# Rotary positions: swapping partitions by transfers from SBUF to SBUF in place of products with a permutation matrix

## What is computed

```python
def apply_rope(t, cos, sin):
    half = t.shape[-1] // 2                      # 32 of the head's 64 channels
    t1, t2 = t[..., :half], t[..., half:]
    return jnp.concatenate([t1 * c - t2 * s_, t2 * c + t1 * s_], axis=-1)

def layer(x, l):
    x = x + 0.5 * rms_norm(swiglu(rms_norm(x, pre1), w_in1, w_out1), post1)
    u = rms_norm(x, mix_pre)
    dq, dk, dv, dz, db, da, sq, sk, sv, gate_a, gate_b = split(u @ mix_w_in)
    y_a = deltanet_branch(dq, dk, dv, dz, db, da, ...)
    y_b = swa_sink_branch(sq, sk, sv, sinks, cos, sin)      # applies apply_rope to sq and sk
    merged = sigmoid(gate_a) * (y_a @ w_branch_a) + sigmoid(gate_b) * (y_b @ w_branch_b)
    x = x + rms_norm(merged @ mix_w_out, mix_post)
    return x + 0.5 * rms_norm(swiglu(rms_norm(x, pre2), w_in2, w_out2), post2)
```

## Time and profile before

| | |
|---|---|
| median of 3 runs | 2424.35 us (2422.82 to 2425.39) |
| the profiled execution | 2424.42 us |
| its span | 2422.6 us |
| granted clock of TensorE, mean | 0.972 |
| TensorE, VectorE, ScalarE, GpSimd busy | 95%, 51%, 32%, 5% |

### The profile page before, as it was taken

How to read it: one execution, slowest core, us unless ns; L and a number is a source line. 1 busy time by engine, 2 the same in 40 slices (tenths; PEclk the granted TensorE clock), 3 DMA queues, 4 the chain that set the end, 5 groups by cost and what they waited for, 6 DMA issues and landing times.

```text
span 2422.6 us, 31002 instructions
## 1 busy us (share of the span) xinstructions
PE 2306.3 (95%) x12232; PEld 1900.0 (78%) x12232; DVE 1225.3 (51%) x1641; ACT 781.7 (32%) x1272; POOL 113.8 (5%) x104
## 2 busy tenths in 40 slices
PE   8999997999899899999899999979998998999997
PEld 6888885788787788888788888857787877888885
DVE  5555325864446565552365553359534465554523
ACT  4333223522443333332243232234134333332321
POOL 0000000131000000000000000002300000000000
PEclk9999998999999999999999999989899999999998
DMA  4332332211122233333222333322111232323332
GB/s 163 97 97 98 99 104 96 66 41 55 51 70 87 105 104 96 96 99 103 84 87 92 99 103 97 104 87 62 45 54 44 79 101 85 117 89 104 104 96 87
DMA packets 58716, 214.79 MB, mean 89 GB/s; under 512 B 6512, under 2 KB 6512, under 8 KB 58096
## 3 DMA queue, kind: packets, MB, share of 16 engines
q1 hardware_dynamic: 57744, 203.82, 26.4%
q0 software_dynamic: 864, 9.44, 1.1%
HBM read 206.94 MB, written 6.29 MB: 88 GB/s over the span
## 4 chain that ended last, share of the span: by engine, by line
PE 73%; issue 15%; DVE 8%; ACT 2%; DMA 1%; POOL 0%; POOLq 0%; DVEq 0%; SPq 0%; ACTq 0%
PE ps L461 22%; PE ps L463 21%; PE ps L462 21%; PE ps L668 1%; DVE tmp L1189 1%; DVE x L1195 1%; DVE wlo L1145 1%; DMA raw<-in_wstream_dram 1%; PE ps L656 1%; PE ps L497 1%; DVE tmp L1343 1%; DVE tmp L1168 1%; ACT whi L850 0%; PE ps L764 0%; PE ps L729 0%
## 5 line engine op out<-in xcount | busy, mean ns | idle before, releaser
L461 PE MATMUL ps<-uhi,whi 128*128 128x512 f32 x2144 | 856.3, 399 | 38.9 <-DVE ulo L1150 18.9
L1145 DVE TENSOR_TENSOR wlo<-raw,whi 128x1024 fp32r<-128x1024 f32 (+1 forms) x384 | 465.9, 1217 | 806.2 <-ACT whi L850 799.1
L462 PE MATMUL ps<-ulo,whi 128*128 128x512 f32 x2144 | 844.7, 394 | 0.0
L463 PE MATMUL ps<-uhi,wlo 128*128 128x512 f32 x2144 | 844.4, 394 | 0.0
L850 ACT ACTIVATE whi<-raw 128x1024 fp32r<-128x1024 f32 (+1 forms) x384 | 397.7, 1040 | 843.6 <-PE ps L463 740.5
L461 PEld LDWEIGHTS ps<-uhi,whi 128*128 128x128 f32 x2144 | 409.0, 191 | 133.0 <-issue 27.2
L463 PEld LDWEIGHTS ps<-uhi,wlo 128*128 128x128 f32 x2144 | 408.6, 191 | 87.3
L462 PEld LDWEIGHTS ps<-ulo,whi 128*128 128x128 f32 x2144 | 409.5, 191 | 83.7 <-issue 0.5
L461 PE MATMUL ps<-hhi,whi 128*128 128x512 f32 x704 | 273.9, 389 | 0.0
L462 PE MATMUL ps<-hlo,whi 128*128 128x512 f32 x704 | 273.9, 389 | 0.0
L463 PE MATMUL ps<-hhi,wlo 128*128 128x512 f32 x704 | 273.9, 389 | 0.0
(11 more groups left out here) (215 smaller groups left out, 1602.0 us busy)
## 6 DMA issues: line engine op xcount, KB each, us to landing
raw<-in_wstream_dram SPq DMA_DIRECT2D x371, 512.0 KB, 3.5
raw<-in_wstream_dram SPq DMA_DIRECT2D x16, 256.0 KB, 2.6
x_home<-x POOLq DMA_DIRECT2D x2, 2048.0 KB, 8.0
x<-x_home POOLq DMA_DIRECT2D x2, 2048.0 KB, 8.7
x<-in_xT_dram SPq DMA_DIRECT2D x4, 512.0 KB, 6.7
out_dram<-x SPq DMA_DIRECT2D x8, 256.0 KB, 2.0
rcs<-in_rope_dram POOLq DMA_DIRECT2D x2, 512.0 KB, 9.9
con<-in_con_dram SPq DMA_DIRECT2D x1, 612.0 KB, 9.2
```

What stands on the lines that cost most here:

```text
L461: pe.matmul(o, lh, bhi, start=first, stop=False)
L462: pe.matmul(o, lh, blo, start=False, stop=False)
L463: return pe.matmul(o, ll, bhi, start=False, stop=last)
L1145: dve.tensor_tensor(wlo[:, s, 0:cols], raw[:, s % RAWS, 0:cols], whi[:, s, 0:cols].bitcast(f32), ALU.subtract) \
```

## The change

The step `rope` leaves TensorE and PSUM. In its place GpSimd issues four transfers per tile ahead of its multiplication by the cosines. Each takes 32 partitions of the tile to the 32 partitions that they change places with, in `tmp` 2 or 3, and counts up a new semaphore, `turned`. VectorE waits for all four and multiplies `tmp` by the sines in place. Since `tmp` 2 and 3 hold the squares of `lst` until then, GpSimd waits for the last of these sums (`l_stat`) ahead of tiles 0 and 1. The signs move into the table of sines. The table of constants loses 128 columns.

```diff
@@ banks_of
-    if k == "rope":
-        return (2 + x % 2,) if x < 4 else (5,)
@@ trunk
+        turned = [sem("turned0", 64 * 3), sem("turned1", 64 * 2)]
@@ TensorE
-                    elif k == "rope":
-                        i, b = step[1], banks_of(step)[0]
-                        use(L, step, b)
-                        pe.wait_ge(tile_read.h, tile_read.at(L, TILE_M + (16 if i < 4 else 17)))
-                        done(pe.matmul(bank(b), con[:, K_ROT:K_ROT + P], attn_in(i), start=True, stop=True), b)
@@ VectorE
                     elif k == "rope":
-                        i, b = step[1], banks_of(step)[0]
-                        ready(step, b)
+                        i = step[1]
                         dve.wait_ge(rope_in.h, rope_in.at(L, 16))
-                        link(L, dve.tensor_tensor(tmp[:, 2 + i % 2, :], bank(b), rcs[:, 1, :], ALU.mult))
+                        dve.wait_ge(turned[i % 2].h, turned[i % 2].at(L, 64 * (i // 2 + 1)))
+                        link(L, dve.tensor_tensor(tmp[:, 2 + i % 2, :], tmp[:, 2 + i % 2, :], rcs[:, 1, :], ALU.mult))
                         dve.wait_ge(rot_cos.h, rot_cos.at(L, i + 1))
                         if i < 4:
                             dve.tensor_tensor(attn_in(i), chunks(tmp[:, 2 + i % 2, :]), chunks(tmp[:, i % 2, :]), ALU.add).then_inc(roped.h, 1)
...
-                        dve.wait_ge(roped.h, roped.at(L, i + 1))
-                        dve.sem_inc(misc_out[b].h, 1)
@@ GpSimd
                         if i >= 2:
                             pool.wait_ge(roped.h, roped.at(L, i - 1))
+                        else:
+                            pool.wait_ge(l_stat.h, l_stat.at(L, 4))
                         pool.wait_ge(tile_read.h, tile_read.at(L, TILE_M + (12 + i if i < 4 else 16) + 1))
+                        for q in range(4):
+                            p, r = 32 * q, 32 * (q ^ 1)
+                            pool.dma_start(chunks(tmp[:, 2 + i % 2, :])[p:p + 32], attn_in(i)[r:r + 32]).then_inc(turned[i % 2].h, 16)
                         pool.tensor_tensor(chunks(tmp[:, i % 2, :]), attn_in(i), chunks(rcs[:, 0, :]), ALU.mult).then_inc(rot_cos.h, 1)
@@ constants
-    for m in range(P):
-        d = m % CH
-        c[m + half if d < half else m - half, K_ROT + m] = -1.0 if d < half else 1.0
...
-    rope = np.stack([np.tile(np.cos(ang), (4, 1)), np.tile(np.sin(ang), (4, 1))], 1)
+    rope = np.stack([np.tile(np.cos(ang), (4, 1)), np.concatenate([-np.sin(ang), np.sin(ang)] * 2)], 1)
```

## The result

The changed kernel takes 2442.24 us (median of 4 runs, 2438.42 to 2445.43), the kernel before 2424.87 beside it (4 runs, 2422.82 to 2426.02). The ratio is 1.0072, with a 95% interval of 1.0054 to 1.0089: slower, by 17 us. The profiled execution took 2441.31, its span is 2439.5 (before: 2422.6), its mean granted clock 0.968 (before: 0.972).

The account below looks back on a forecast made before the run. TensorE was taken to bound the kernel, with VectorE's rotary latency on the path in stage 16. Sum: 2424.42 + 11.9 (chunk 18 later) + 2 (contention) + 1.6 (clock) - 3.2 (tile 4) = 2436.7, said as 2437; range 2426 to 2455.

Parts of the forecast that it names:

- stage 16: Inside invd, TensorE waits until 535 for PSUM bank 7, idle for 8 us; Z comes at about 534.5 instead of 528.55.
- t0: End of GpSimd's new wait for l_stat, when VectorE's eqs starts: 523.95 in layer 0, 1726.84 in layer 1.
- VectorE's idle time of 5 us ahead of tile 0: Sign in the changed profile: VectorE idle for 5 us ahead of tile 0's multiplication until a DMA.
- The price of an issue: Time each transfer's issue holds GpSimd's queue: 0.8 us taken, between 0.55 and 1.1 to 1.2.
- Rival 1: The number of pieces costs nothing, an issue takes 0.55 us: 2428.7, without contention 2426.7; chance 0.17.
- GpSimd's mask sets the pace in stage 17: Second mask for invp ready at t0 + 20.9, later than TensorE's arrival; chunk 18 starts 5.2 and 6.7 us later.
- d: Price of one transfer's issue in GpSimd's queue, taken as 0.8 us.
- Contention: VectorE and GpSimd working on SBUF together: one loss of 0.9 us in each layer, 2 us in the sum.
- tile 3's addition not later than the mask: Stage 17 on VectorE: tile 3 landed t0 + 18.1, done t0 + 19.5, unless landing takes over 4 us.
- The source of the multiplication: VectorE's rotary multiplication only changes its source from PSUM to SBUF: nothing by itself.
- Tile 4: Ahead of chunk 20: wait for bank 5 and product go, 1.6 us saved per layer; the transfers have cover.
- The clock: A stretch of 8 matmuls at the low clock, 1.6 us added in layer 0 alone; bounds nothing and 6 us more.

Follow-up runs that it names:

- the version with `l_stat` on SyncE: Changed kernel with SyncE issuing the transfers and amask at the end of stage 15, tmp 2 and 3 again behind l_stat: 2421.4 us, ratio 0.9992.
- the kernel with dummy transfers: Kernel before, products kept, plus 20 small dummy transfers per layer issued by GpSimd behind the wait for l_stat: 2449.01 us, ratio 1.0107.
- both edits: Changed kernel with transfers early into tmp 4 and 5 (no wait for l_stat) and amask at the end of stage 15: 2427.33 us, ratio 1.0008.

## Why the prediction was right, and where its working failed

The prediction was slower, 2437 in a range of 2426 to 2455; measured 2442.2. It put the loss at 12.3 us, and the span grew by 16.9. The direction and stage 16 were right by the mechanism; that the time came near owes something to luck. Step by step:

1. **Stage 16 held**, by two errors that cancel. I put Z at 534.5; it came at 535.28, with t0 itself 0.8 later (524.75 against 523.95), so on the spot. But tile 1's multiplication started at t0 + 8.2 and not t0 + 9.2, since the issues were cheaper, and VectorE then needed 2.4 us in place of 1.4, since the addition took 1.66. The wait was predicted as 8 and is 8.2 and 8.19. VectorE's idle time of 5 us ahead of tile 0 is 5.29 (4.50 in layer 1). The runs agree that the start counts: the late start costs 9 us where nothing else is in play (the version with `l_stat` on SyncE).
2. **The price of an issue was over-sized:** 0.8 taken, 0.584 measured, with 256 pieces: 3.5 us too much in each layer. With 32 pieces (tile 4) it is 0.506. Eight times the pieces cost 0.08 us. Rival 1 was right in its condition. Such a price is what the Trainium skill (DMA: Bandwidth & Descriptors, "Anatomy of one DMA — SWDGE (gpsimd) path") leads one to expect, and these rows agree with it.
3. **"GpSimd's mask sets the pace in stage 17" is the step that failed.** With d = 0.584 the second mask was ready at 544.0, t0 + 19.3, and `invp` hardly waited for it (0.57). What came last was VectorE's `vtm`, done at t0 + 27.6.
4. **Contention was under-sized**, and this is the larger error. I put one loss of 0.9 us in each layer. On the five operations of stage 17 it is 13.3 − 4.0 = 9.3 us in each layer; this is time of VectorE, and what reached chunk 18 of it is less. I had called tile 3's addition not later than the mask; it was ready at 551.7, against 543.5 by my sum. Moving `amask` gave 10 us back.
5. **The source of the multiplication, "nothing by itself", doesn't hold for the operation.** The multiplication that reads PSUM takes 0.69 beside a running `attnT` (in the kernel with dummy transfers, and in layer 1 of the kernel before); the one that reads SBUF takes 1.77 and 2.83 in stage 17. Over 0.69 each, that is 3.2 of the 9.3 us. The swap by TensorE had kept this operation out of the contention; the change put it in. What that costs the kernel isn't shown: no run changes the source alone, and an operation that isn't held can leave the wait to the addition behind it. The kernel with dummy transfers, which still reads PSUM, is only 3.6 us per layer ahead at chunk 18, and landing and dearer issues are in that too.
6. **Tile 4 held**: 1.6 us per layer predicted, 1.5 measured alone.
7. **The clock.** I added 1.6 us in layer 0. Behind the wait of 6.6, chunk 18 started at 1.2 GHz, 0.43 us per matmul, in both layers: 9 to 10 matmuls in layer 0 and 6 in layer 1. Before, it did so in layer 1 only the earlier trace rows. At 0.2 us per matmul that is 2.0 in layer 0, and layer 1, with 8 such matmuls before, gained 0.4: 1.6 in sum, and the term held. It is within the 18.1 and 17.4 us from chunk 18 to 20. Chunk 17 was at that clock too, for 6 matmuls in layer 0 (12 before) and 10 in layer 1 (none before), but `vtm` ended later than that chunk.

So steps 2 and 4 erred in opposite directions. Chunk 18 came at t0 + 28.4 instead of the t0 + 23.7 of my sum: 9.4 us more in both layers, of which 2 were in the forecast as contention. With an issue at 0.584 the sum would have put it at t0 + 20.2; it came 8.2 us later than that in each layer, and moving `amask` took back 5.4 and 4.2 of them. The rest of the span gave 3.0 back. The forecast was near because the first error covered part of the second; its direction rests on step 1, which the experiments bear out.

The rule behind step 4 is this, as the rows show it: an operation of VectorE with two SBUF inputs and one of GpSimd that reads SBUF don't share. The rotary one ends as if it had waited for GpSimd's to end (0.55 us behind it, four times above), in one case for two of them in a row. The Trainium skill (SBUF — State Buffer, "Who interferes with whom") states that: an operation of VectorE with two SBUF inputs contends with one of GpSimd that reads SBUF, one with at most one SBUF input doesn't. Both halves agree with the rows. The prediction took the size of the loss from one row instead of asking who stands beside whom after the move. The additions of 1.91 and 1.80 us in layer 1 of the kernel before would have said that `amask` is the neighbour to ask about.

What stays open: why the kernel with the dummies took a median of 2449.0 where its profiled execution took 2441.8 (the executions above 2450 had a mean granted clock of 0.964, the profiled one 0.968), the 3.0 us that the rest of the span gave back, and why VectorE's operations were slow within a run of GpSimd's issues in some cases and not in others.

## What to carry to other kernels

When data are moved by DMAs in place of TensorE, count whom the issuing engine's later work will now run beside, and whether an operation that read PSUM reads SBUF afterwards: here moving one step of GpSimd's out of the way gave back 10 of the 17 us lost. Ask which queue has spare time at that place, and whether the buffer is free before the last wait; issued by SyncE into a buffer of its own, with GpSimd's masks moved out of the way, the same swap made the kernel 0.5% faster (2412.2 us, ratio 0.9952) instead of 0.7% slower. Edits can need each other: with GpSimd issuing, the early start (4 us) and the masks (10) simply added up to 15, while SyncE as the issuer gave 11 us with the masks in place and 15 with the masks moved.

## What the runs showed of the hardware

- GpSimd's issue of a transfer of 32 partitions took 0.584 us with 256 pieces and 0.506 with 32; on SyncE the same took 0.610 and 0.591 (medians). From issue to landing it was 2.0 us (1.9 to 3.6) and 2.7 (2.1 to 3.7) for 64 KB from SBUF to SBUF.
- A row of back-to-back instructions on GpSimd can hold one operation of VectorE through several of them: 7.51 us for a split of 1.22, past four instructions and through the memsets between. The Trainium skill (SBUF — State Buffer, "Who interferes with whom") speaks of an exclusive lock, held by whoever issues first for the whole instruction (it says so of VectorE's modes with two ports), and of an instruction of GpSimd that only writes SBUF as no rival; by that the split would have run in the first memset at 537.5. The row says it didn't, and the row decides. It need not go that way: with both edits a split that started at 538.76 ended at 541.84, 1.09 us behind the first mask's end, so it ran from that mask's memset on.
- Under the same conditions GpSimd mostly kept its own durations (1.29, 1.29, 1.28, 2.35), and so won the contest; the fifth, which was running when the split ended, took 3.21 in place of 2.35 to 2.7.
- Within a run of four issues by GpSimd, with no other work of GpSimd beside it, an operation of VectorE with two SBUF inputs took up to 1.68 us in place of 0.69: 1.55 after the change (layer 1), 1.46 with the masks moved (layer 0), 1.68 with the dummy transfers (both layers). Others in such a run took 0.69. The cause is not shown.
